# Sums of squares of the delta rule's queries and keys as rounded products, placed behind the first rotary unit

## What is computed

```python
qkv = jax.nn.silu(centred_depthwise_conv(qkv, conv_w))
q, k, v = jnp.split(qkv, 3, axis=-1)
q, k, v = heads(q), heads(k), heads(v)
l2n = lambda t: t * lax.rsqrt(jnp.sum(t * t, axis=-1, keepdims=True) + NORM_EPS)
q = l2n(q) * GDN_HEAD_DIM ** -0.5
k = l2n(k)
```

## Time and profile before

| | |
|---|---|
| median of three runs | 1926.64 us |
| lowest and highest | 1926.19 and 1926.86 us |
| profiled execution, span from first to last instruction | 1926.1 us |
| TensorE busy | 1912.5 us, 99% of the span |
| GpSimd busy | 1545.7 us, 80% |
| ScalarE busy | 1081.6 us, 56% |
| VectorE busy | 710.4 us, 37% |
| TensorE's granted clock | 1.000 over the span |

### The profile page before, as it was taken

How to read it: one execution, slowest core, us unless ns; L and a number is a source line. 1 busy time by engine, 2 the same in 40 slices (tenths; PEclk the granted TensorE clock), 3 DMA queues, 4 the chain that set the end, 5 groups by cost and what they waited for, 6 DMA issues and landing times.

```text
span 1926.1 us, 28361 instructions
## 1 busy us (share of the span) xinstructions
PE 1912.5 (99%) x11293; PEld 1685.0 (87%) x11293; DVE 710.4 (37%) x1428; ACT 1081.6 (56%) x1439; POOL 1545.7 (80%) x1228
## 2 busy tenths in 40 slices
PE   9999999999999999999999999999999999999998
PEld 7888899988888888889999888888999998888887
DVE  2221767521311232128574231113577632122112
ACT  6645684456644575456735565446666667445443
POOL 6998786666899799979776759997767787888995
PEclk9999999999999999999999999999999999999999
DMA  8554543143555565555322535555443444445552
GB/s 321 179 204 175 197 154 132 45 177 130 219 197 183 187 227 205 179 193 186 143 88 105 187 125 207 188 196 202 152 160 145 148 160 153 175 177 206 196 182 103
DMA packets 48661, 331.50 MB, mean 172 GB/s; under 512 B 5393, under 2 KB 6289, under 8 KB 10514
## 3 DMA queue, kind: packets, MB, share of 16 engines
q1 hardware_dynamic: 44208, 314.61, 44.3%
q10 hardware_dynamic: 4322, 15.09, 2.3%
HBM read 328.63 MB, written 1.05 MB: 171 GB/s over the span
## 4 chain that ended last, share of the span: by engine, by line
PE 97%; ACT 1%; DVE 1%; issue 0%; ACTq 0%; DVEq 0%
PE bank L1966 20%; PE bank L1935 16%; PE bank L1936 16%; PE bank L1937 16%; PE bank L1970 10%; PE bank L2074 2%; PE bank L2098 2%; PE bank L2076 1%; PE bank L2412 1%; PE bank L2428 1%; PE bank L2040 1%; PE bank L2534 1%; PE bank L2513 1%; PE bank L2674 1%; PE bank L2088 0%; ACT arena L422 0%
## 5 line engine op out<-in xcount | busy, mean ns | idle before, releaser
L391 POOL TENSOR_TENSOR wlo<-raw,whi 128x512 fp32r<-128x512 f32 x1184 | 1501.0, 1305 | 332.5 <-ACT whi L422 331.9
L422 ACT ACTIVATE whi<-raw 128x2048 fp32r<-128x2048 f32 (+1 forms) x299 | 567.5, 1901 | 188.8 <-PE bank L1937 168.8
L422 ACT ACTIVATE arena<-bank 128x512 f32<-128x512 f32 (+4 forms) x389 | 210.3, 551 | 445.2 <-PE bank L1970 268.4
L1966 PE MATMUL bank<-uT,whi 128*128 128x512 f32 x1632 | 408.2, 392 | 0.0
L1966 PEld LDWEIGHTS bank<-uT,whi 128*128 128x128 f32 x1632 | 296.3, 189 | 55.0
L1970 PEld LDWEIGHTS bank<-uT,wlo 128*128 128x128 f32 x1632 | 222.6, 190 | 15.9
L1970 PE MATMUL bank<-uT,wlo 128*128 128x256 f32 x1632 | 227.6, 282 | 0.0
L1935 PE MATMUL bank<-uT,whi 128*128 128x256 f32 x768 | 222.5, 290 | 0.0
L1936 PE MATMUL bank<-uT,whi 128*128 128x256 f32 x768 | 217.1, 283 | 0.0
L1937 PE MATMUL bank<-uT,wlo 128*128 128x256 f32 x768 | 217.1, 283 | 0.0
L1935 PE MATMUL bank<-whi,uT 128*128 128x512 f32 (+1 forms) x416 | 160.8, 387 | 0.0
(11 more groups left out here) (321 smaller groups left out, 2702.0 us busy)
## 6 DMA issues: line engine op xcount, KB each, us to landing
raw<-in_w SPq DMA_DIRECT2D x295, 1024.0 KB, 4.8
rows<-in_rows ACTq DMA_DIRECT2D x22, 512.0 KB, 4.7
raw<-in_w SPq DMA_DIRECT2D x4, 512.0 KB, 6.7
arena<-in_mem ACTq DMA_DIRECT2D x2, 1024.0 KB, 7.8
x<-in_x SPq DMA_DIRECT2D x2, 512.0 KB, 5.2
arena<-in_amask ACTq DMA_DIRECT2D x1, 576.0 KB, 6.4
out<-x SPq DMA_DIRECT2D x1, 512.0 KB, 2.7
out<-arena SPq DMA_DIRECT2D x1, 512.0 KB, 2.7
```

The costliest lines, as they stand in the source:

```text
L391: r = pool.tensor_tensor(wlo[n % LAND][:, k], raw[n % LAND][:, k], whi[n % RING][:, k].bitcast(F32), ALU.subtract)
L422: return act.activation(o, i, f, **k)
L1966: pe.matmul(both, w[0][:, c], parts[:, :, k, :], start=start and k == 0, stop=False)
```

## The change

Four things are changed, in both layers.

1. The squares are rounded. Behind Square, ScalarE has a second drain and a Copy of the four tiles into `sq_hi`, in float32r. Only this Copy reports `squares`.
2. VectorE makes the rest `sq_lo = sq - sq_hi`, 1024 elements per partition for each group, between `convolve(4)` and `convolve(5)`, and reports `squares_lo`.
3. TensorE sums with two single-pass products instead of one product in plain float32, ones x `sq_hi` and ones x `sq_lo`, with a rounded matrix of ones, which ScalarE copies once in a layer in front of its copy of `ab`.
4. The square sums stand behind the first rotary unit `proj_T(0)` instead of in front of it, and wait for `squares_lo`.

`sq_lo` lies where the rotated queries and keys are written later, `sq_hi` where the output gates are written later.

```diff
+        sq_hi = nc.alloc_sbuf_tensor_at("sq_hi", [P, 8, 256], F32R, offset=arena_base + 4 * 9264)
+        sq_lo = nc.alloc_sbuf_tensor_at("sq_lo", [P, 8, 256], F32R, offset=arena_base + 4 * 6192)
+        ones_r = nc.alloc_sbuf_tensor_at("ones_r", [P, P], F32R, offset=arena_base + 4 * 2048)
...
+                fn(ones_r[:, :], ones, AF.Copy)
                 fn(ab[0], small[:, S_AB:S_AB + P], AF.Copy).then_inc(sems["ab_hi"], 1)
...
                         act.drain()
-                        fn(sq[:, 4 * g:4 * g + 4, :], cout[:, 4 * g:4 * g + 4, :], AF.Square).then_inc(sems["squares"], 1)
+                        k = slice(4 * g, 4 * g + 4)
+                        fn(sq[:, k, :], cout[:, k, :], AF.Square)
+                        act.drain()
+                        fn(sq_hi[:, k, :], sq[:, k, :], AF.Copy).then_inc(sems["squares"], 1)
...
                 convolve(4)
+                for g in range(2):
+                    k = slice(4 * g, 4 * g + 4)
+                    dve.wait_ge(sems["squares"], p.count("squares"))
+                    tt(sq_lo[:, k, :], sq[:, k, :], sq_hi[:, k, :].bitcast(F32), ALU.subtract).then_inc(sems["squares_lo"], 1)
                 convolve(5)
...
-                for j in range(4):
-                    if j % 2 == 0:
-                        pe.wait_ge(sems["squares"], p.count("squares"))
-                    acquire(2 + j, "act")
-                    pe.matmul(bank[2 + j][:, :], ones, arena[:, 512 * j:512 * (j + 1)], start=True, stop=True)\
-                        .then_inc(sems[f"act_bank{2 + j}"], 1)
+                def square_sums():
+                    for j in range(4):
+                        if j % 2 == 0:
+                            pe.wait_ge(sems["squares_lo"], p.count("squares_lo"))
+                        acquire(2 + j, "act")
+                        k = slice(2 * j, 2 * j + 2)
+                        pe.matmul(bank[2 + j][:, :], ones_r[:, :], sq_hi[:, k, :], start=True, stop=False)
+                        pe.matmul(bank[2 + j][:, :], ones_r[:, :], sq_lo[:, k, :], start=False, stop=True)\
+                            .then_inc(sems[f"act_bank{2 + j}"], 1)
...
                 proj_T(0, "rotated", uT)
+                square_sums()
                 proj_T(1, "rotated", uT)
```

## The result

| | before | changed |
|---|---|---|
| median of ten runs | 1927.57 us | 1934.42 us |
| lowest | 1926.19 us | 1933.2 us |
| highest | 1936.4 us | 1945.24 us |
| span of the profiled execution | 1926.1 us | 1932.6 us |
| mean granted clock over the span | 1.000 | 0.996 |

The changed kernel is slower by the factor 1.004 (95% interval 1.003 to 1.0051), which is 7.7 us (5.8 to 9.8); the two medians as such differ by 6.85 us. The forecast was +4.3 us. The direction was right and the size was not: by the ratio, what happened is nearly twice what the sum said.

The account below looks back on a forecast made before the run. TensorE's instruction stream, busy 99%, was taken as the bound. Per layer -4.53 + 1.82 + 1.6 + 2.25 + 1.0 = +2.15 us; two layers, +4.3 on 1926.64, gave 1930.9 us, range 1929.1 to 1934.6.

Parts of the forecast that it names:

- ScalarE, 2.27 us: ScalarE's two added copies of squares, each behind a drain: 2.27 us in a layer, none of it hidden.
- The two waits behind it: TensorE's later waits: 2.25 us for g_ready and 1.0 us for run_lo in a layer; decay sums 2.15 us late.
- TensorE's new products, 0.227 us each: Eight rounded 128x512 products for the square sums on TensorE, 1.82 us in a layer, replacing 4.53 us.
- VectorE's subtraction: Each 1024-element subtraction making low parts: 3.1 to 3.2 us, bounds 1.2 and 3.25; TensorE waits 1.6 us for them.
- a longer wait for the low parts: Rival at the square sums: a subtraction over 4.1 us delays the third sum's Ln and everything behind; chance 0.02.
- The clock: TensorE's clock in the main forecast: no fall, so no cost added.
- Rival B: TensorE's clock falls after idling for g_ready, adding 1.9 to 4.8 us in a layer: 1934.6 to 1940 us; chance 0.12.
- rival B's milder case: Only the half unit up to the decay sums runs at 1.2 GHz: +1.9 us in a layer, 1934.6 us.
- The offset: Whole kernel: the median of runs, 1926.64 us, lies 0.5 us above the profiled span of 1926.1 us.
- Rivals A: TensorE's later mixer waits at L2495 and L2412 give back 0.85 us in each layer: 1929.1 us; chance 0.10.
- C: ScalarE's chain absorbs the copies, so TensorE's stream decides: 1924.5 us, or 1921.2 with quick subtractions; chance 0.06.

Follow-up runs that it names:

- e2: Changed kernel without VectorE's subtractions, rounded squares summed twice; 1935.82 us against 1926.82 us for the kernel before, ratio 1.0046.
- e12: Changed kernel without subtractions, rounded squares summed twice, plus 16 dummy products before TensorE's wait for g_ready; 1932.25 against 1926.98 us for the kernel before, ratio 1.0025.
- e4: Changed kernel with the squares held in PSUM instead of SBUF; 1936.08 us against 1926.82 us for the kernel before, ratio 1.0046.
- e3: Changed kernel with each subtraction cut into four pieces of 256 elements; one execution, 1943.36 us.
- e8: Changed kernel with squares in PSUM and ScalarE's queue reordered, g_ready and run_lo made earlier on VectorE; 1930.67 against 1928.05 us for the kernel before, ratio 1.0015.
- e5: Changed kernel with dummy products, 8 and 4, before TensorE's two waits for the low parts; 1934.73 against 1926.82 us for the kernel before, ratio 1.004.
- e1: Kernel before with only its plain float32 square sums moved behind the first rotary unit, nothing rounded; 1931.39 against 1926.82 us, ratio 1.002.
- e9: Kernel before with plain float32 square sums behind the first rotary unit and e8's order of ScalarE's and VectorE's queues; 1932.88 us, ratio 1.0027.

## Why the prediction was wrong

**ScalarE, 2.27 us: right.** Run is late by 2.26 and 2.27 us where nothing else interferes (e2, e12), and no part of it is hidden. The two waits behind it, for g_ready and for run_lo, are where the forecast put them. With the clock kept up the decay sums are 2.07 us late, forecast 2.15.

**TensorE's new products, 0.227 us each: right** at full clock (0.24 from start to start in the first two sums).

**VectorE's subtraction: this is the first step that failed.** The prediction said "Twice the size gives 1.2 us at best and 3.25 us at most; I take 3.1 to 3.2". It took 6.15 and 2.31 us. The 3.25 was no upper bound: it doubled a row, L1365, whose time was not made of elements alone. The work is 1.225 us at most (e4); the rest is the wait for the other engine, and e3 shows that it does not shrink with the work. L1365's 1.62 us leave room for a wait of less than one GpSimd instruction (1.29 us), in a stretch where VectorE's own instructions follow each other. So it is with the second subtraction, with the later pieces of e3 and with the rotations of e8. The first subtraction came after VectorE had been idle, beside a GpSimd run without gaps, and about four of GpSimd's instructions went by. It is tempting to say that VectorE's idle time decides, but a row of the kernel before speaks against it: L1359, a subtraction of 128x128 with both inputs in SBUF, came after 1.49 us of idle VectorE, in a GpSimd run without gaps (207.69 to 231.05), and took only 0.57 us. What decides stays open. The Trainium skill ("SBUF — State Buffer", Who interferes with whom) says that the later one fully blocks until the first finishes. That it blocks fully agrees with the trace (the subtraction ended 1.08 us behind GpSimd's end at 257.15); that it waits for one instruction, as I read the page, does not.

I gave "a longer wait for the low parts", from 4.1 us on, 2 in 100. It happened: 8.38 us for both made the third and fourth Ln wait. Its price, with the clock kept up, is 3.14 - 2.07 = 1.07 us in a layer (e5 in layer 1 against e12); the forecast had nothing for it.

**The clock: the second step that failed. The forecast put it at nothing, because no row showed a fall. Rival B was right in kind, but I put it in another place and set it against the forecast instead of on top of it.** It fell behind the wait for the low parts (2.04 us idle), not behind the one for g_ready. Its price is 3.87 - 3.14 = 0.73 us in a layer, though it lasts 6.8 us in layer 0 and 3.4 in layer 1: most of it is hidden, since ScalarE's queue decides when g_ready and run_lo come; what is not hidden is that the last two sums take longer and Ln waits for them. A quick subtraction would not have saved the forecast: without it (e2) or with it at 1.225 us (e4) the clock fell behind the longer wait for g_ready, and the kernel was no faster. The Trainium skill ("TensorE: Matmul & The Clock Gate", Why this matters for your kernels) warns of idle gaps between bursts. The traces agree that every fall in the mixer stood behind a new wait of TensorE, of 1.01 us or more, but most of these waits are shorter than the gap that the page names, and behind others of 1.01, 1.1, 2.38 and 2.4 us the clock stayed up; here the measurement decides.

Together 2.07 + 1.07 + 0.73 = 3.87 us in a layer, 7.7 in all. The three terms are differences between the same runs and must add up. ScalarE's own rows bear out the last two: its Ln waits 0.92 us in e5, and 1.42 + 0.17 us in the changed kernel, 0.67 more. The forecast had the first term. That the measured median, 1934.42, nearly meets the 1934.6 of rival B's milder case is luck: B had 1.9 us in a layer from the clock at g_ready alone, and what came on top was 1.07 us of late sums and 0.73 us of clock at another place.

**The offset.** The 0.5 us between span and median was taken from two different executions. The changed kernel's profiled execution has its own time, 1934.46 us, 1.9 us over its span of 1932.6. The forecast added its 4.3 us to the median, so this changed nothing.

**Rivals A and C** did not happen: the waits at L2495 and L2412 are as long as before under new line numbers, and ScalarE's chain took up nothing.

**What stays open.** In e1, e5, e8 and e9 the same wait (1.01, 1.1, 2.38 and 2.4 us) was followed by a fall of the clock in one layer and not in the other; no run here says what decides. And the start of the program varies by some 2 us between executions. The forecast took from the clock row that the kernel before ran at full speed everywhere, but near its start the spacing of the products says otherwise: four of 128x512 at 12.37 us (L2247) take 1.69 us together, so they start 0.43 us apart, like the sums at 1.2 GHz above, while the row has 1.00 there. Why the two differ, no run here says. It does not touch the mixers, where products of the same form keep their 0.12 us.

## What to carry to other kernels

A saving on the busiest engine is worth nothing until the queue that feeds its next wait is looked at, instruction by instruction: here 2.7 us of products were bought with 2.3 us of a queue without a gap, and the same rounding pays once that queue is reordered and the squares lie in PSUM. Waits and a slow clock are not alternatives in a forecast; a new wait of a microsecond on TensorE should carry the clock's price on top, with a chance, since the fall did not come every time. Do not scale the time of an instruction that was measured beside another engine with which it takes turns: for an upper bound take the work at its free rate and add the longest run of the other engine as the wait, or take an operand from PSUM.

## What the runs showed of the hardware that I had not expected

- A VectorE subtraction with both inputs in SBUF, given out while GpSimd worked through 5 us of such subtractions without a gap, ended only 1.08 or 0.29 us behind GpSimd's pause, whether it had 1024 elements (6.15 us) or 256 (5.34 us). With one input in PSUM it took 1.225 us beside the same work.
- Once in, VectorE takes turns with GpSimd (pieces of 256 elements in 1.48 us in e3), and GpSimd pays too: its instructions beside the second subtraction took 1.53 and 2.26 us instead of 1.29.
- The granted clock of TensorE went from 2.4 to 1.2 GHz behind single idle times of 1.01, 1.1, 2.04, 2.38 and 3.68 us, and stayed at 2.4 behind others of 1.01 (e1), 1.1 (e5), 2.38 (e8) and 2.4 us (e9), each in the other layer of the same execution.
